# A gated delta layer with its block-diagonal factors stored as 64 columns a head, and its squares summed on VectorE

## The reference

```python
def gdn_chunk(S, q, k, v, beta, g):
    gc = jnp.cumsum(g, axis=-1)
    decay = jnp.exp(jnp.where(tril, gc[..., :, None] - gc[..., None, :], -jnp.inf))
    kb = k * beta[..., None]
    M = jnp.einsum('bhid,bhjd->bhij', kb, k) * jnp.where(strict, decay, 0.0)
    rhs = jnp.concatenate([v * beta[..., None], kb * jnp.exp(gc)[..., None]], axis=-1)
    uw = triangular_solve(M + jnp.eye(L), rhs, left_side=True, lower=True, unit_diagonal=True)
    u, w = uw[..., :DV_A], uw[..., DV_A:]
    v_new = u - einsum('bhld,bhde->bhle', w, S)
    attn = einsum('bhid,bhjd->bhij', q, k) * decay
    o = einsum('bhld,bhde->bhle', q * exp(gc)[..., None], S) + einsum('bhij,bhje->bhie', attn, v_new)
    S_new = S * exp(gl)[..., None] + einsum('bhld,bhle->bhde', k * exp(gl - gc)[..., None], v_new)
```

## Time and profile before

| | us |
|---|---|
| median of 3 runs | 3906.15 (3904.22 to 3907.92) |
| span of the profiled execution | 3905.3 |
| TensorE busy | 3687.1 (94%) |
| VectorE busy | 1749.4 (45%) |
| ScalarE busy | 1326.2 (34%) |
| `delta`, all of it | 449 |

### The profile page before, as it was taken

How to read it: one execution, slowest core, us unless ns; L and a number is a source line. 1 busy time by engine, 2 the same in 40 slices (tenths; PEclk the granted TensorE clock), 3 DMA queues, 4 the chain that set the end, 5 groups by cost and what they waited for, 6 DMA issues and landing times. The chain is left out here.

```text
span 3905.3 us, 62624 instructions
## 1 busy us (share of the span) xinstructions
PE 3687.1 (94%) x24668; PEld 2632.8 (67%) x24668; DVE 1749.4 (45%) x4469; ACT 1326.2 (34%) x3423; POOL 165.4 (4%) x191
## 2 busy tenths in 40 slices
PE   6999999969999888999999998999999999799998
PEld 3777777758888544666666445677767767677775
DVE  2443434446665234655555222221221122499996
ACT  1111111136665225655555001222122111355553
POOL 0000000011110000000000000000000000000100
PEclk8999999979999899999999999999999999899999
DMA  7111111132210011000001664111111111433433
GB/s 288 46 53 60 45 45 45 44 103 85 86 49 31 22 50 33 28 17 17 17 11 54 224 215 159 70 61 57 72 62 59 70 70 64 180 114 145 156 129 116
DMA packets 114815, 317.49 MB, mean 81 GB/s; under 512 B 30040, under 2 KB 48392, under 8 KB 109384
## 3 DMA queue, kind: packets, MB, share of 16 engines
q1 hardware_dynamic: 111864, 288.48, 20.1%
q0 software_dynamic: 2768, 26.47, 2.3%
HBM read 205.16 MB, written 109.74 MB: 81 GB/s over the span
## 5 line engine op out<-in xcount | busy, mean ns | idle before, releaser
L2352 PE MATMUL e_p<-e_hT,w_ahead 128*128 128x128 f32 x3264 | 411.4, 276 | 3.2 <-DMA shared<-w_in_o 3.2
L2352 PEld LDWEIGHTS e_p<-e_hT,w_ahead 128*128 128x128 f32 x3264 | 390.0, 193 | 11.3 <-issue 11.3
L535 PEld LDWEIGHTS a_p<-a_hT,w_even 128*128 128x128 f32 x3264 | 369.7, 193 | 9.4 <-issue 7.7
L535 PE MATMUL a_p<-a_hT,w_even 128*128 128x128 f32 x3264 | 369.9, 276 | 1.3 <-DVE a_hT L318 1.3
L550 PE MATMUL a_p<-w_even,a_hT 128*128 128x512 f32 (+2 forms) x1024 | 370.4, 522 | 0.0
L550 PEld LDWEIGHTS a_p<-w_even,a_hT 128*128 128x128 f32 x1024 | 194.0, 191 | 164.9 <-issue 115.8
L1675 DVE TENSOR_REDUCE q_mx<-q_sps 128x1 f32<-128x512 f32 (+4 forms) x320 | 181.4, 583 | 215.2 <-PE q_sps L1516 214.4
L2744 PE MATMUL h_b<-h_w,h_oT 128*128 128x512 f32 x512 | 236.6, 596 | 0.0
L2199 PE MATMUL c_b<-shared,c_oc 128*128 128x512 f32 x512 | 224.6, 598 | 9.2 <-DMA c_oc<-scr_ob 9.2
L2303 ACT ACTIVATE e_r<-e_p 128x512 f32<-128x512 f32 x66 | 39.4, 597 | 518.5 <-PE e_p L2358 298.7
L1604 ACT ACTIVATE q_P<-q_sps,q_mx 128x512 f32<-128x512 f32 (+4 forms) x320 | 190.6, 602 | 19.6 <-DVE q_mx L1680 14.9
(11 more groups left out here) (458 smaller groups left out, 6047.0 us busy)
## 6 DMA issues: line engine op xcount, KB each, us to landing
scr_qkg<-e_r SPq DMA_DIRECT2D x68, 512.0 KB, 2.6
h_rq<-scr_qkg SPq DMA_DIRECT2D x17, 2048.0 KB, 10.7
scr_iz<-e_r SPq DMA_DIRECT2D x34, 512.0 KB, 2.6
scr_qkv<-a_cv SPq DMA_DIRECT2D x17, 768.0 KB, 3.2
d_sc<-scr_qkv SPq DMA_DIRECT2D x17, 768.0 KB, 4.3
wa<-w_ada SPq DMA_DIRECT2D x8, 1536.0 KB, 16.2
w_ahead<-w_ada POOLq DMA_DIRECT2D x8, 1536.0 KB, 7.7
w_ahead<-w_in_o POOLq DMA_DIRECT2D x6, 2048.0 KB, 8.9
```

The costliest lines, as they stand in the source:

```text
L535: mm = pe.matmul(bank[g][:, (c % 4) * P:(c % 4 + 1) * P], w[:, k, c * P:(c + 1) * P], hT[:, p, k, :], start=k == 0, stop=k == KD - 1)
L2352: mm = pe.matmul(bank[n % 4][:, c * P:(c + 1) * P], w[k][:, a:a + P], hT[:, p, k, :], start=k == 0, stop=k == KD - 1)
```

## The change

- M, MT, T0, U0, T, U, XI, A, the masks and the two decay matrices are stored with 64 columns a head: rows 0 to 63 hold the first chunk's block, rows 64 to 127 the second's. The predicated copies, the copies by ScalarE and the exponentials work on 256 columns instead of 512. T and U share one PSUM bank (B1 for the first three levels, B2 for the last two), and one copy takes both.
- `products` makes the two diagonal blocks alone, as pairs with 64 stationary and 64 moving columns; `M_columns` is done by 64x64 matmuls with the identity; `within` by 64x64 pairs with 128 moving columns. `solve` makes w with 64x128 weights and 64 moving columns, the first chunk into BX and the second into B2, and u with 64x64 pairs.
- `exponents` takes the difference of the gates once, from a second copy of the gates that SP loads with two more DMAs a tile, and makes both decay matrices from it, in three instructions instead of eight.
- `squares` writes the squares of a whole bank with one activation and no `accum_out`; `roots` on VectorE then sums 8 x 128 columns in one reduction.
- At the start, GpSimd builds the identities by an addition of two halves, and two clears of PSUM banks by VectorE are gone.

```diff
-        lowT, maskD, maskE = sb("d_lowT", [P, 5, P]), sb("d_maskD", [P, P]), sb("d_maskE", [P, P])
+        lowT, low0, level0 = sb("d_lowT", [P, 5, CH]), sb("d_low0", [P, CH]), sb("d_level0", [P, CH])
+        masks, DE = sb("d_masks", [P, 2, CH]), sb("d_DE", [P, 3, H, CH])
...
-        EB, Dm, Em = sb("d_EB", [P, 4, H, P]), sb("d_Dm", [P, H, P]), sb("d_Em", [P, H, P])
-        vb, kb, kd, qe, A, MT = (sb(f"d_{n}", [P, 4, H, P]) for n in ("vb", "kb", "kd", "qe", "A", "MT"))
-        M, T0, U0, XI = sb("d_M", [P, H, P]), sb("d_T0", [P, H, P]), sb("d_U0", [P, H, P]), sb("d_XI", [P, 5, H, P])
-        T, U = sb("d_T", [P, 2, H, P]), sb("d_U", [P, 2, H, P])
+        EB = sb("d_EB", [P, 4, H, P])
+        vb, kb, kd, qe = (sb(f"d_{n}", [P, 4, H, P]) for n in ("vb", "kb", "kd", "qe"))
+        A, MT = sb("d_A", [P, 4, H, CH]), sb("d_MT", [P, 4, H, CH])
+        M, T0, U0, XI = sb("d_M", [P, H, CH]), sb("d_T0", [P, H, CH]), sb("d_U0", [P, H, CH]), sb("d_XI", [P, 5, H, CH])
+        TU = sb("d_TU", [P, 2, 2, H, CH])
...
             def load_g(t):
                 rows = scr["gc"][t * H:(t + 1) * H, :].rearrange("h t -> (h t)").unsqueeze(0).to_broadcast([P, H * P])
                 sp.dma_start(flat(gcB[:, t % 4, :, :]), rows).then_inc(g_in[t % 4], 16)
+                for own in CHUNKS:
+                    sp.dma_start(gcC[own, t % 4, :, :], scr["gc"][t * H:(t + 1) * H, own].unsqueeze(0).to_broadcast([CH, H, CH])).then_inc(g_in[t % 4], 16)
...
             def squares(a):
                 act.wait_ge(R["qkvT"], a + 1)
-                for h in range(2 * H):
-                    bank = (A0, A1)[h // H]
-                    u_ = act.activation(sqj[:, h, :], bank[:, h % H * P:(h % H + 1) * P], ACT.Square, accum_out=ss8[:, a % 2, h:h + 1])
+                since(act, R["sum8"], a)
+                for n, bank in enumerate((A0, A1)):
+                    u_ = act.activation(flat(sqj[:, n * H:(n + 1) * H, :]), bank[:, :], ACT.Square)
...
                 act.activation(flat(EB[:, a % 4, :, :]), flat(gcB[:, a % 4, :, :]) if a else BO[:, :], ACT.Exp)
-                act.activation(flat(Dm[:, :, :]), flat(Dm[:, :, :]), ACT.Exp, scale=-1.0)
-                act.activation(flat(Em[:, :, :]), flat(Em[:, :, :]), ACT.Exp).then_inc(R["ex"], 1)
+                act.activation(DE[:, 0:2, :, :], DE[:, 0:2, :, :], ACT.Exp).then_inc(R["ex"], 1)
...
             def first(b, n):
                 act.wait_ge(R["TU1"], 3 * b + n + 1)
-                act.copy(flat(T[:, b % 2, :, :]), BT[:, :])
-                act.copy(flat(U[:, b % 2, :, :]), BU[:, :]).then_inc(R["K1"], 1)
+                act.copy(TU[:, b % 2, :, :, :].rearrange("p a h t -> p (a h t)"), B1[:, :]).then_inc(R["K1"], 1)
...
             def second(c, n):
                 act.wait_ge(R["TU2"], 2 * c + n - 2)
                 if n == 3:
-                    act.copy(flat(T[:, c % 2, :, :]), BT[:, :])
-                act.copy(flat(U[:, c % 2, :, :]), BU[:, :]).then_inc(R["K2"], 1)
+                    k_ = act.copy(TU[:, c % 2, :, :, :].rearrange("p a h t -> p (a h t)"), B2[:, :])
+                else:
+                    k_ = act.copy(TU[:, c % 2, 1, :, :], half(B2, 1))
+                k_.then_inc(R["K2"], 1)
 
...
             def solved(c):
                 act.wait_ge(R["wu"], c + 1)
                 since(act, R["vn"], 2 * c)
-                act.copy(flat(wT[:, :, :]), BX[:, :]).then_inc(R["wTc"], 1)
+                for own, bank in zip(CHUNKS, (BX, B2)):
+                    k_ = act.copy(wT[:, :, own], half(bank, 0))
+                k_.then_inc(R["wTc"], 1)
...
                 pe.wait_ge(R["qkTc"], a + 1)
                 pe.wait_ge(R["vb"], a + 1)
                 for h in range(H):
-                    pe.matmul(A2[:, h * P:(h + 1) * P], qkT[:, H + h, :], qkT[:, H + h, :], start=True, stop=True)
-                    mm = pe.matmul(A0[:, h * P:(h + 1) * P], qkT[:, H + h, :], qkT[:, h, :], start=True, stop=True)
+                    for bank, right in ((A2, H + h), (A0, h)):
+                        for own in CHUNKS:
+                            mm = pe.matmul(half(bank, 0)[own, h, :], qkT[:, H + h, own], qkT[:, right, own], start=True, stop=True)
...
             def M_columns(a):
                 pe.wait_ge(R["M"], a + 1)
                 for h in range(H):
-                    mm = pe.transpose(A1[:, h * P:(h + 1) * P], M[:, h, :], ident[:, :])
+                    for own in CHUNKS:
+                        mm = pe.matmul(half(A1, 0)[own, h, :], M[own, h, :], ident[own, own], start=True, stop=True)
                 mm.then_inc(R["MTt"], 1)
...
-            def by_chunks(bank, h, left, right):
-
-
-                for c in range(2):
-                    own = slice(c * CH, (c + 1) * CH)
-                    mm = pe.matmul(bank[own, h * P + c * CH:h * P + (c + 1) * CH], left[own, own], right[own, own], start=True, stop=True)
+            def by_chunks(to, h, left, right):
+
+                for own in CHUNKS:
+                    mm = pe.matmul(to[own, h, :], left[own, h, :], right[own, h, :], start=True, stop=True)
                 return mm
 
-            def X_of(x, T_of, done):
...
-            def TU_of(n, U_of, done):
+            def TU_of(bank, n, U_of, done):
                 for h in range(H):
                     if n < 4:
-                        by_chunks(BT, h, U_of[:, h, :], XI[:, n, h, :])
-                    mm = by_chunks(BU, h, XI[:, n, h, :], U_of[:, h, :])
+                        by_chunks(half(bank, 0), h, U_of, XI[:, n, :, :])
+                    mm = by_chunks(half(bank, 1), h, XI[:, n, :, :], U_of)
                 mm.then_inc(done, 1)
...
             def solve(c):
                 pe.wait_ge(R["K2"], 2 * c + 2)
                 pe.wait_ge(R["kbd"], c + 1)
                 pe.wait_ge(R["vb"], c + 1)
                 since(pe, R["og"], c)
+                U = TU[:, c % 2, 1, :, :]
                 for h in range(H):
-                    pe.matmul(BX[:, h * P:(h + 1) * P], kb[:, c % 4, h, :], U[:, c % 2, h, :], start=True, stop=True)
-                    mm = pe.matmul(BO[:, h * P:(h + 1) * P], U[:, c % 2, h, :], vb[:, c % 4, h, :], start=True, stop=True)
+                    for own, bank in zip(CHUNKS, (BX, B2)):
+                        pe.matmul(half(bank, 0)[:, h, :], kb[own, c % 4, h, :], U[own, h, :], start=True, stop=True)
+                    for own in CHUNKS:
+                        mm = pe.matmul(heads(BO)[own, h, :], U[own, h, :], vb[own, c % 4, h, :], start=True, stop=True)
...
             def within(t):
                 pe.wait_ge(R["A"], t + 1)
                 for h in range(H):
-                    mm = pe.matmul(BO[:, h * P:(h + 1) * P], A[:, t % 4, h, :], vn[:, h, :], start=False, stop=h == H - 1, skip_group_check=True)
+                    for own in CHUNKS:
+                        mm = pe.matmul(heads(BO)[own, h, :], A[own, t % 4, h, :], vn[own, h, :], start=False, stop=h == H - 1, skip_group_check=True)
                 mm.then_inc(R["o_ps"], 1)
...
             def roots(a):
                 dve.wait_ge(R["ss"], a + 1)
+                dve.tensor_reduce(ss8[:, a % 2, :], sqj[:, :, :], AX, ALU.add).then_inc(R["sum8"], 1)
+                dve.wait_ge(R["sum8"], a + 1)
                 dve.scalar_tensor_tensor(out=ss8[:, a % 2, :], in0=ss8[:, a % 2, :], scalar=EPS, in1=dk8[:, :], op0=ALU.add, op1=ALU.mult).then_inc(R["ssm"], 1)
...
             def exponents(a):
-                rows = gcB[:, a % 4, :, :] if a else heads(BO)
+                rows = bc(gc[:, a, :], CH)
                 if a:
-                    dve.wait_ge(g_in[a % 4], (a // 4 + (1 if a % 4 else 0)) * 16)
+                    dve.wait_ge(g_in[a % 4], (a // 4 + (1 if a % 4 else 0)) * 48)
+                    dve.tensor_tensor(DE[:, 2, :, :], gcC[:, a % 4, :, :], rows, ALU.subtract).then_inc(R["diff"], 1)
                 else:
                     dve.wait_ge(R["gcB0"], 1)
                     dve.wait_ge(R["tl"], 1)
-                for h in range(H):
-                    dve.scalar_tensor_tensor(out=Dm[:, h, :], in0=rows[:, h, :], scalar=gc[:, a, h:h + 1], in1=maskD[:, :], op0=ALU.subtract, op1=ALU.max)
-                    v = dve.scalar_tensor_tensor(out=Em[:, h, :], in0=rows[:, h, :], scalar=gc[:, a, h:h + 1], in1=maskE[:, :], op0=ALU.subtract, op1=ALU.min)
-                v.then_inc(R["DE"], 1)
+                    for own in CHUNKS:
+                        v = dve.tensor_tensor(DE[own, 2, :, :], heads(BO)[own, :, own], rows[own], ALU.subtract)
+                    v.then_inc(R["diff"], 1)
+                dve.wait_ge(R["diff"], a + 1)
+                dve.scalar_tensor_tensor(out=DE[:, 0, :, :], in0=DE[:, 2, :, :], scalar=-1.0, in1=over_heads(masks[:, 0, :], H), op0=ALU.mult, op1=ALU.min)
+                dve.tensor_tensor(DE[:, 1, :, :], DE[:, 2, :, :], over_heads(masks[:, 1, :], H), ALU.min).then_inc(R["DE"], 1)
...
             def into(dst, mask, src, at, done):
                 dve.memset(hold[:, at:at + 1], 0.0)
```

(14 more changed lines are left out.)

58 lines of the change are left out of this document (32 added, 26 removed).

## The result

The changed kernel takes 3895.36 us (median of 20 runs, 3891.95 to 3900.06) against 3904.98 us for the kernel before on the same chip (20 runs, 3900.86 to 3907.93): 0.9977 of the time, interval 0.9971 to 0.9983. It is 9.6 us faster. The forecast was faster by 21: the direction and the range hold, and more than half of the gain is missing.

The account below looks back on a forecast made before the run. TensorE's own work was taken to bound the middle of the gated delta stage. Fourteen steps at -1.0 us (-14), the start (-2.3, -2.1, -2.0) and the end (-0.5) made -21 us: 3885 us, range 3864 to 3899.

Parts of the forecast that it names:

- The first wait: TensorE's 0.67 us wait a step for VectorE's factor copy at `TU_second` goes; net gain 0.6 us.
- `products`: TensorE group in each step: eight side-by-side pairs take 1.08 us instead of 1.98, saving 0.9.
- `within`: TensorE group in each step: four 64x64 pairs take 0.9 us instead of four full matmuls, saving 0.1.
- The second wait: TensorE's wait ahead of `products` for ScalarE's copies of transposed queries and keys: stays at 0.55 us a step.
- The reduction: VectorE's new sum of 1024 elements ahead of `roots`: 1.23 us, covered by 0.65 us before `into_state`.
- Rival 4: VectorE's reduction over 1.9 us delays `into_state`, each further us costing 17 us; 0.07 together with unforeseen waits.
- `solve`: TensorE group ending each step: 2.5 us, 0.6 more than now, with eight shape changes at 0.09; bounds 1.5 and 4.3.
- Gotcha 1: Skill rule: different row tiles can't share a PSUM bank at once; priced 3.5 us a step, given no weight.
- The end: Last stretch of the delta stage: two `solve` +1.2 against shorter hops -1.7, so -0.5 us.
- The start: First three steps of the delta stage, partly at 1.2 GHz: -2.3, -2.1 and -2.0 us.
- rival 5: TensorE's clock in the start stays up as waits shorten: 3 us more gained, inside the range; no chance given.
- Rivals 1 to 3: `solve` cheap at 1.5 us (0.28); w chunks in line, 3.3 (0.12); in line with full-price shape changes, 4.3 (0.06).

Follow-up runs that it names:

- longer exponents: The changed kernel with three more 256-element VectorE instructions in `exponents` that nobody reads: 3912.11 us (one run).
- `products` alone: The kernel before with only `products` changed, to make the two diagonal blocks alone in 64-column pairs: 3895.82 us, 0.9979.
- grouped `solve`: The changed kernel with the matmuls of `solve` reordered, all four u pairs first, then all four w pairs: 3874.23 us, 0.9928.
- filled end: The changed kernel with eight unread matmuls added in the two TensorE waits of step t = 15: 3891.17 us, 0.9968.
- `X_first` ahead: Grouped `solve` with `X_first(b, 2)` moved ahead of `X_second(c, 4)` on TensorE: 3882.45 us; with eight unread matmuls added in step t = 15: 3876.15 us.

## Why the prediction was right and wrong

All that stands ahead of `solve` was right: by the forecast's terms it had to start at 23.42 - 1.6 - 1.89 = 19.93 us of the step, and it starts at 19.96. Point by point:

- *The first wait*: forecast -0.6 (7.28 to 6.54, less 0.14 given back by the update), measured -0.48, with the small wait for the state's update that was named as next in line. The run with longer exponents shows that VectorE's shorter chain is the cause.
- *`products`*: forecast 1.08, measured 1.08. What the forecast did not say is that 0.4 of its 0.9 are only kept because VectorE's work is shorter too, as `products` alone shows.
- *`within`*: 0.1 forecast, 0.16 measured.
- *The second wait*: stays at 0.55, as said. ScalarE's 54 us less in the middle buy nothing.
- *The reduction*: 1.23 forecast, 1.22 measured; with or without it the step is 22.90 us. Rival 4 is out.
- *`solve`*: the mis-sized term of the middle. The forecast of 2.5 had the w pairs and u pairs side by side at 0.22 each and 0.09 for each change of shape, "the low end, since part of a load can hide under the pair before it". That low end is the step that failed. By the forecast's own terms, the pairs at 1.78 and 8 changes at the measured 0.15 make 3.0, and 2.94 was measured; the grouped `solve`, with two changes, would be 2.1 and is 2.01. So the price of a pair was right and the price of a change was not: the rows of the group boundaries said 0.10 to 0.20, and 0.09 lay below them. 14 x 0.44 = 6 us of the 10.5 that are missing are this choice. The four u pairs, both halves in one bank, take 0.97 us for eight matmuls of 128 columns, 0.24 a pair where the earlier trace rows have 0.22 for one matmul of 128 columns, so they run side by side. What the Trainium skill states in "TensorEngine Tiling (Array Packing)", section Tiling Modes, that a change of mode drains TensorE, agrees with the runs, which put it at 0.15 us; the rule of the same page's Gotcha 1 on one PSUM bank does not show in them. The forecast's price for that rule was wrong in any case: 0.44 for each of four heads is 1.8 us a step, not 3.5.
- *The end*: forecast -0.5, measured +5.4. This is the second step that failed: I counted two `solve` and some hops and never asked what the clock would do, which was considered for the start alone. Its term was put at nothing without a reason, and the fall behind step 15 cost 3.9 us (10.6 us where the filled end takes 6.7). The two `solve` gave back 1.05 each and not 0.6, which is 0.9, and the shorter hops were worth 0.6 and not 1.7: together the 5.9. That the fillers keep the clock up is shown by the profiles of two pairs of kernels, and by the runs of the pair with `X_first` ahead (6.3 us, of which its end has 3.9); in the changed kernel the gain is 2.6 us by the distances to the kernel before, and not clear of noise. Why the clock fell is not shown: the grouped `solve` has the same two waits with TensorE busy for 2.44 of 5.00 us, the kernel before has waits of 1.49 and 0.90 us with 2.61 of 5.00, and in both it held. What decides between these cases stays open; that a fall comes or not by where the execution happens to stand, as the rival of the filled end has it, is not ruled out.
- *The start*: forecast -6.4, measured -8.6. The third step won 3.3 us where 2.0 were forecast, the first two 0.3 each more than forecast. This fits rival 5, the clock, which no run tests by itself: the profile of before has it falling in the third step (first line, before), that of after not (second line):

```profile
889.60:896.40 6.80, 5.77 (x86) 5.46 (x87) 2.17 (x5) 4.81 (x14) 0.00 (x0) 0.54 0.00 0
```

```profile
879.00:895.50 16.50, 12.82 (x296) 10.93 (x296) 8.37 (x26) 8.46 (x23) 1.75 (x1) 1.00 0.23 74
```

Together: 6.7 us too much forecast in the middle, 5.9 in the end, 2.2 too little in the start: 10.4 of the 10.5 that the stage is short of. Rivals 1 to 3 were all about `solve` and are decided: not cheap, not in line, and with 2.94 below the value from which the change would lose (3.8 in the forecast; its own 2.5 + 1.2 makes 3.7). The medians differ by 9.6 us and the profiles by 12.3; runs of the changed kernel scatter over 8 us, and no run here says which of its ends does that.

## What to carry to other kernels

When full matmuls are replaced by pairs of small ones, count the changes of tile shape, and price each as the group boundaries of the trace show it; then sort the matmuls so that one shape follows another once, which here was worth 20 us, twice the change itself: 14 of them in the middle, and some 3.5 from a clock that did not fall, which this order is not shown to ensure. A saving on the engine that bounds is whole only as long as the others keep up, so look for who is late next, as VectorE was here twice (M with `products` alone, and M again when the first wait was filled). In a pipeline's tail, where the bounding engine begins to wait, read the granted clock before and after: a few unread matmuls in two waits took away a fall that costs 4 us, and gained a clear 6 us in one of the two kernels in which it had fallen.
